# Small attention weights three tiles later in the load order, and the sum over seven squared blocks moved to GpSimd for the last three norms

## The reference

```python
h = jnp.concatenate([meta, x], axis=1)
for layer in range(DEPTH):                      # 2
    u = rmsnorm(h, attn_norm[layer])
    ... = jnp.split(u @ w_in[layer], offsets, axis=-1)
    o_mla = mla_branch(..., w_uq, ..., w_ukv, ...)
    o_gla = gla_branch(..., w_g2, ...)
    o_hgrn = hgrn2_branch(...)
    mixed = gates[0] * (o_mla @ w_mla_o) + gates[1] * (o_gla @ w_gla_o) + gates[2] * (o_hgrn @ w_hgrn_o)
    h = h + mixed @ w_out[layer]
    u = rmsnorm(h, ffn_norm[layer])
    if layer % 2 == 0:
        h = h + swiglu(u, w_gate, w_up, w_down)     # d_ff 2816
    else:
        h = h + moe_swiglu(u, ...)                  # top 2 of 8 experts, 3584 wide

def rmsnorm(x, g):
    return x * rsqrt(mean(x * x, axis=-1) + EPS) * g
```

## Time and profile before

| | |
|---|---|
| time, median of 3 runs | 1955.93 us (1954.07 to 1957.28) |
| profiled execution, its time | 1951.37 us |
| its span in the trace | 1949.5 us |
| TensorE busy | 96% of the span |
| VectorE busy | 79% |
| ScalarE busy | 66% |
| GpSimd busy | 2% |
| HBM traffic | 243 GB/s over the span |

### The profile page before, as it was taken

The page is one execution under the profiler, slowest core; times in us unless marked ns, Lnnn a source line. Parts: engine busy times, 40 slices in busy tenths (PEclk is TensorE's granted clock), DMA queues, the critical chain, the costliest instruction groups (busy, mean ns, idle before and its releaser), DMA issues.

```text
span 1949.5 us, 30232 instructions
## 1 busy us (share of the span) xinstructions
PE 1865.6 (96%) x11056; PEld 1620.7 (83%) x11056; DVE 1538.6 (79%) x1898; ACT 1294.5 (66%) x1640; POOL 43.1 (2%) x42
## 2 busy tenths in 40 slices
PE   7998999999979998999899999999999999999998
PEld 6988888899978887888788888888888888888886
DVE  5868787555438688776898998989989889798897
ACT  5776766444336775864676777767777677776775
POOL 0000003000000000012000000000000000000001
PEclk9999999999999999999999999999999999999999
DMA  5323324455443332336499998989989999998994
GB/s 190 130 92 126 108 98 142 141 174 173 160 176 108 114 116 96 119 120 242 170 370 347 352 371 331 369 350 355 367 350 356 346 353 371 351 349 346 357 369 171
DMA packets 83702, 474.14 MB, mean 243 GB/s; under 512 B 10480, under 2 KB 10768, under 8 KB 40352
## 3 DMA queue, kind: packets, MB, share of 16 engines
q1 hardware_dynamic: 83616, 472.98, 65.0%
HBM read 471.89 MB, written 1.05 MB: 243 GB/s over the span
## 4 chain that ended last, share of the span: by engine, by line
PE 73%; DVE 12%; ACT 9%; issue 5%; DMA 1%; POOL 0%; DVEq 0%; ACTq 0%; SPq 0%; POOLq 0%
PE bank L1690 9%; PE bank L1695 9%; PE bank L1691 9%; PE bank L1414 8%; PE bank L1416 7%; PE bank L1415 7%; PE bank L1707 5%; PE bank L1713 5%; PE bank L1708 5%; DVE mlo L1211 2%; DVE lo L872 2%; PE bank L1659 1%; ACT hi L593 1%; PE bank L1722 1%; PE bank L1409 1%
## 5 line engine op out<-in xcount | busy, mean ns | idle before, releaser
L1211 DVE TENSOR_TENSOR mlo<-mraw,mhi 128x2048 fp32r<-128x2048 f32 x283 | 642.2, 2287 | 70.3 <-ACT mhi L806 69.3
L806 ACT ACTIVATE mhi<-mraw 128x2048 fp32r<-128x2048 f32 x283 | 539.6, 1916 | 104.6 <-PE bank L1695 53.9
L1414 PE MATMUL bank<-UH,hi 128*128 128x272 f32 (+1 forms) x1376 | 416.4, 303 | 18.8 <-DVE UL L885 8.6
L1416 PE MATMUL bank<-UH,lo 128*128 128x272 f32 (+1 forms) x1376 | 397.5, 289 | 0.0
L1415 PE MATMUL bank<-UL,hi 128*128 128x272 f32 (+1 forms) x1376 | 396.2, 288 | 0.0
L593 ACT ACTIVATE hi<-raw 128x1024 fp32r<-128x1024 f32 (+1 forms) x220 | 229.3, 1043 | 133.0 <-PE bank L1416 123.9
L1690 PE MATMUL bank<-mhi,xh 128*128 128x512 f32 x768 | 303.3, 395 | 3.4 <-DVE xl L1296 3.4
L1691 PE MATMUL bank<-mhi,xl 128*128 128x512 f32 x768 | 299.9, 390 | 0.0
L872 DVE TENSOR_TENSOR lo<-raw,hi 128x1024 fp32r<-128x1024 f32 (+1 forms) x220 | 266.2, 1223 | 41.6 <-ACT hi L593 41.1
L1414 PEld LDWEIGHTS bank<-UH,hi 128*128 128x128 f32 x1376 | 260.7, 189 | 32.9 <-issue 27.3
L1415 PEld LDWEIGHTS bank<-UL,hi 128*128 128x128 f32 x1376 | 261.8, 190 | 1.6 <-issue 0.5
(11 more groups left out here) (342 smaller groups left out, 2584.5 us busy)
## 6 DMA issues: line engine op xcount, KB each, us to landing
mraw<-in_w_exp SPq DMA_DIRECT2D x336, 1024.0 KB, 4.8
raw<-in_w_dense SPq DMA_DIRECT2D x212, 512.0 KB, 3.2
raw<-in_w_dense SPq DMA_DIRECT2D x8, 384.0 KB, 3.0
wuq<-in_w_uq SPq DMA_DIRECT2D x2, 1024.0 KB, 7.2
mixed<-in_x SPq DMA_DIRECT2D x2, 512.0 KB, 5.9
wukv<-in_w_ukv SPq DMA_DIRECT2D x2, 512.0 KB, 7.6
out<-acc SPq DMA_DIRECT2D x4, 256.0 KB, 3.0
C<-in_consts SPq DMA_DIRECT2D x1, 576.0 KB, 7.9
```

The costliest lines, as they stand in the source:

```text
L806: A_(mhi[k % MHI][:], mraw[k % MRAW][:], ACT.Copy).then_inc(mhi_made, 1)
L1211: TT(mlo[k % MRAW][:], mraw[k % MRAW][:], mhi[k % MHI][:].bitcast(F32), ALU.subtract).then_inc(mlo_made, 1)
L1414: MM(ps, h, xh_, start=first, stop=False)
L1416: return MM(ps, l, xh_, start=False, stop=last)
```

## The change

Three edits. The small weights are issued ahead of `gk` 0 and not ahead of `gd` 0, with the same wait in layer 1. GpSimd adds `gt[:, m, :]` into `gt[:, 0, :]` for m from 1 to 6, as soon as ScalarE has made each square, and counts that in the new semaphore `sq_added`. TensorE's matmuls between the tiles go; `norm(phase)` of norms 1 to 3 now issues two, one for `gt[:, 0, :]`, which holds the sum of blocks 0 to 6, and one for block 7. Norm 0 stays as it was.

```diff
-                if kind == "gd":
+                if kind == "gk" and i == 0:
...
                     sp.dma_start(wuq[:], A["w_uq"][layer]).then_inc(small_landed, 16)
...
-            for layer, kind, i in jobs:
+            for g, (layer, kind, i) in enumerate(jobs):
+                if g in squares_at and squares_at[g][1]:
+                    phase, m = squares_at[g]
+                    pool.wait_ge(norm_sq, KD * phase + m + 1)
+                    if m > 1:
+                        pool.wait_ge(sq_added, (KD - 2) * (phase - 1) + m - 1)
+                    pool.tensor_tensor(gt[:, 0, :], gt[:, 0, :], gt[:, m, :], ALU.add).then_inc(sq_added, 1)
...
-                for k in range(KD) if phase == 0 else (KD - 1,):
+                for k in range(KD) if phase == 0 else (KD - 2, KD - 1):
...
             def sum_squares(phase, m):
+                if phase and m < KD - 1:
+                    pe.wait_ge(sq_added, (KD - 2) * phase)
+                    return MM(bank[2][:, 0:T], ones, gt[:, 0, :], start=True, stop=False)
                 pe.wait_ge(norm_sq, KD * phase + m + 1)
...
                     stream(g, half)
-                    if half == 1 and g in squares_at:
-                        sum_squares(*squares_at[g])
```

More of the change, by code:

```diff
@@ L409, in bass_hybrid_trunk @@
         small_used = sem("small_used")
-        zeroed = sem("zeroed")
+        zeroed, sq_added = sem("zeroed"), sem("sq_added")
         hi_made, lo_made = sem("hi_made"), sem("lo_made")
```

## The result

The changed kernel takes **1933.74 us** (median of 4 runs, 1931.56 to 1937.05) against 1955.66 us: ratio 0.9892, 95% interval 0.9877 to 0.9907, so 21.9 us or 1.1% less. The profiled executions took 1951.37 us before and 1931.56 now, 19.8 us less. The forecast was 1938.8 us for the median, and 17.15 us less for the profiled execution.

The account below looks back on a forecast made before the run. TensorE's own work was taken as the bound, except for a stall at the turn to layer 1. 7.86 + 0.55 + 8.74 = 17.15 us off the 1955.93 us median gave 1938.8 us, range 1933 to 1943.

Parts of the forecast that it names:

- The stall: Turn from layer 0 to layer 1: ScalarE no longer waits for late tile `gd` 0, 7.86 us less.
- The room: At the turn `gd` 0, landing in 3.2 us, would be there some 2 us before it is wanted.
- The last sum at norm 2: TensorE's last sum at norm 2 takes 0.74 us and not 1.29: 0.55 us less, bounds 0 and 0.55.
- step from norm 1 to norm 2: Norm 2's last sum should take what norm 1's does, as idle lengths agree within 2 us; gives the 0.55 us.
- the forecast's 8.41: Gain at norm 2, the turn to layer 1: 7.86 us of stall and 0.55 us of the last sum.
- The sums: Between the tiles of both layers, 19 matmuls off TensorE's path at 0.46 us each: 8.74 us less, bounds 8.1 and 8.9.
- the cover: VectorE's idle time per tile, 1.25 us in the new rhythm, hides what GpSimd's additions cost; without it 8.3 us.
- the 0.46 us feared for each `split_lo`: VectorE's `split_lo`, 1.22 us alone and 1.68 beside GpSimd, may lose 0.46 us for an addition, hidden in idle time.
- The stall did not stay: Rival at the turn: something else holds `gd` 0 or ScalarE until about 580, only the sums count: 1947.2 us; chance 0.05.
- the experts' pace did not swallow the gain: Rival in the experts: the weight stream sets the end, time stays within 0.2% (1952 to 1960 us); chance 0.02.
- no tile got another pace: Rival at the `wout` tiles: longer `split_lo` or square holds the next tile, 5.5 us less gain, 1944.3 us; chance 0.07.
- nothing became slower: Rival: blocking between VectorE and GpSimd lands on TensorE at each of 18 additions, 30.2 us, so 1969 us; chance 0.02.

Follow-up runs that it names:

- the move alone: The kernel before with only the small weights moved ahead of `gk` 0 in both layers, TensorE's sums as before: 1945.92 us, ratio 0.9953.
- TensorE kept busy: Six more float32 matmuls into an unused bank at norms 1 and 2, on the changed kernel with early table load and early block 7 square: 1933.09 us.
- the early table load: The changed kernel with ScalarE's table load at layer 1's start issued ahead of the high half of `gd` 0: 1936.68 us against 1935.62.

## Why the prediction was right, point by point

*The stall.* Right to the hundredth: 7.86 us in the move alone, with `hi`'s free buffer 0.09 us after the last product as the next thing late. That `gd` 0 alone was to blame was shown by moving the weights by one tile. The room, put at 2 us, was smaller: the tile took 4.1 us to land and not 3.2, and lay ready 1.6 us before it was wanted in the move alone and 1.3 in the change (issued 560.12, wanted 565.45).

*The last sum at norm 2.* 0.74 us and not 1.29, a gain of 0.55 as forecast, but in part by luck. The same program took 1.00 us in its second profile and 0.74 in its third, and with the move alone it stayed at 1.29 in both profiles, though it began 2.9 us after the last product there as in the change; with GpSimd's work times six, the same program at this place, it took 1.3 us too. An idle length like norm 1's does not fix the clock of the sum. The forecast's step from norm 1 to norm 2 was therefore not safe, and its lower bound of 0 was reached in other runs.

*What was not in the sum:* at norm 2 I left out the first tile of layer 1. From its first product to ScalarE's reading of it, it took 577.84 - 571.87 = 5.97 us and before 592.74 - 587.57 = 5.17. ScalarE's reading in the changed kernel, then before:

```profile
577.84 0.40 ACT L644 ACTIVATE dqT<-bank 128x272 f32<-128x272 f32 x1 [2.18 <-PE bank L1425]
```

```profile
592.74 0.40 ACT L638 ACTIVATE dqT<-bank 128x272 f32<-128x272 f32 x1 [1.38 <-PE bank L1416]
```

Before, the clock was low from 577.6 to 591.3, 3.7 us into this tile; in the changed kernel from 570.6 to 577.4, 5.5 us into it. So 0.80 of the 8.41 us went back in this pair, and the runs with TensorE kept busy show that it is the clock. It is no fixed price of the change either: in its second profile the clock was low from 569.3 to 576.1, and the tile took 5.18 us. Turn and first tile together took 20.39 us before and 12.78, 12.25 and 12.89 in the three profiles of the change, so 7.5 to 8.1 us of the forecast's 8.41 stay.

*The sums.* 3.26 us in the feed-forward part for 7, and 2.75 and 2.73 in the two layers once the places with another clock are taken out (3.18 - 0.69 + 0.26 in layer 0, 1.78 + 0.80 - 1.58 + 1.73 in layer 1, from the steps in the lead of `split_hi`): 8.74 in all, as forecast. In layer 0 each of the 13 sums is by itself a step of 0.45 to 0.47 us in that lead. Norm 1, with its new matmul in the place of block 6's, took what it did.

*GpSimd and VectorE.* Nobody waits for the additions. The forecast feared 1.68 us for one and saw up to 1.56; the cover held at six times the work. Its reading that both engines become longer is wrong: of two that meet, the one that starts first keeps its time, and the other is held. In the kernel before, where the addition starts first (the timelines of GpSimd and of VectorE):

```profile
313.31 0.78 POOL L567 TENSOR_TENSOR mixed<-mixed,gt 128x272 f32<-128x272 f32 x1 [2.24 <-DVE gt L952]
...
313.50 1.67 DVE L872 TENSOR_TENSOR lo<-raw,hi 128x1024 fp32r<-128x1024 f32 x1
```

The addition takes its 0.78 us, and `split_lo` ends 1.08 us behind it, nearly the 1.22 us that it takes alone. Where `split_lo` starts first it takes its 1.22 us (322.35 to 323.57), and the addition ends 0.62 us behind it (324.19). With GpSimd's work times six both happen in turn: an addition holds the `split_lo` of 343.12, which ends at 344.77, and that holds the next addition, which ends 0.50 us later:

```profile
343.64 1.63 POOL L565 TENSOR_TENSOR spare<-gt 128x272 f32<-128x272 f32 x1
```

By the Trainium skill ("SBUF — State Buffer", "Who interferes with whom") the two share one pair of ports, and whichever starts first keeps it for its whole instruction. The traces agree, in each of these three meetings. In the changed kernel the new additions never hold a `split_lo`: among layer 0's `wout` tiles they start as it ends (340.69 against 340.75), among the `fd` tiles it starts first and takes its 1.22 us. So the 0.46 us feared for each `split_lo` was not paid at all.

*The median.* The forecast of 1938.8 us is 5 us above it, in the range. 17.15 us were forecast and 19.8 measured between the profiles; the 2.7 us are 0.86 at the start and 2.34 in the experts, less what the layers lost, and none of it is of the change. The other runs of the same kernel gave 1935.62 and 1935.93, with ratios whose intervals (0.9887 to 0.9917, 0.9902 to 0.9929) hold the forecast's 0.9912; that of the first pair (0.9877 to 0.9907) lies just beyond it.

*The rivals.* The stall did not stay, the experts' pace did not swallow the gain (first expert product 17.48 us earlier, none lost after), no tile got another pace, and nothing became slower.

## What to carry to other kernels

A queue of loads that all wait in order hides a cost in its order: one load with a wait of its own (here for a bank to be empty) makes everything behind it late, so ask which of the tiles behind it is the first to be wanted, and put that one ahead. When TensorE is the bound, a matmul between its tiles is worth what the chain gives it, here 0.46 us each; VectorE and GpSimd, both with idle time at each tile, took the work equally well. Count the stages of two traces one by one before you read a difference of the whole: here norm 1 came again to 0.01 us in three profiles of the change (5.38 and 5.39), while the profiled executions lay up to 5.7 us apart. Where two engines slow each other, look at single instructions: a mean or a merged row hides that one of the two keeps its time.

## What the runs showed of the hardware that was not expected

The same program had its granted clock lowered at different places from run to run, and with it layer 1 took 330.06 or 332.38 us. Short gains are therefore seen in the trace and not in the time: the early table load won 1.3 us at the turn and nothing in the median. Even a stage holds some of it: the turn took 6.81, 7.07 and 6.80 us in three profiles of the change, and the tile behind it 5.97, 5.18 and 6.09, by where the low stretch of the clock lay. Six spare matmuls at each of two norms kept the clock at its upper level there and shortened what stands behind them by 1.0 and 0.9 us against the same kernel without them, with no change of the result.
